# Recurrence of a bidirectional RWKV-7 mixer: turns in quadrants, side work spread over the levels, key factors on GpSimd

## What is computed

```python
def _rwkv_step(S, inp):
    r, w, kk, kka, kt, v = inp
    sk = jnp.einsum('bhij,bhj->bhi', S, kk)
    S = S * w[:, :, None, :] - sk[..., None] * kka[:, :, None, :] + v[..., None] * kt[:, :, None, :]
    return S, jnp.einsum('bhij,bhj->bhi', S, r)
```

## Time and profile before

| | us |
|---|---|
| median of 3 runs | 5085.33 |
| lowest and highest | 5072.62, 5091.82 |
| the profiled execution | 5078.06 |
| its span on the core | 5076.7 |
| TensorE busy | 4573.2 |
| VectorE busy | 1419.8 |
| ScalarE busy | 1174.9 |
| GpSimd busy | 270.6 |

### The profile page before, as it was taken

The page is one execution under the profiler, slowest core; times in us unless marked ns, Lnnn a source line. Parts: engine busy times, 40 slices in busy tenths (PEclk is TensorE's granted clock), DMA queues, the critical chain, the costliest instruction groups (busy, mean ns, idle before and its releaser), DMA issues. The chain is left out here.

```text
span 5076.7 us, 86103 instructions
## 1 busy us (share of the span) xinstructions
PE 4573.2 (90%) x37006; PEld 2463.5 (49%) x37006; DVE 1419.8 (28%) x3516; ACT 1174.9 (23%) x2541; POOL 270.6 (5%) x418
## 2 busy tenths in 40 slices
PE   8999999989998899786999997996888888769998
PEld 6775444434444344543444443444666666534333
DVE  1032110020001221533222225133555555532223
ACT  2032111012101222423222221033333333321111
POOL 0000000000002002102000000022000000010000
PEclk9999999999999899997999998998999999979999
DMA  3143111121122113422777773233000000029998
GB/s 132 67 159 117 66 67 71 66 93 69 66 83 78 50 46 101 139 78 97 294 285 291 285 285 139 91 143 95 28 28 28 28 28 9 3 96 400 407 408 342
DMA packets 257924, 679.81 MB, mean 134 GB/s; under 512 B 23600, under 2 KB 66464, under 8 KB 257296
## 3 DMA queue, kind: packets, MB, share of 16 engines
q1 hardware_dynamic: 234048, 608.24, 32.4%
q0 software_dynamic: 23504, 66.07, 4.3%
HBM read 644.76 MB, written 26.74 MB: 132 GB/s over the span
## 5 line engine op out<-in xcount | busy, mean ns | idle before, releaser
L2197 PE MATMUL bank<-ring,arena 128*128 128x512 f32 x2592 | 1128.8, 596 | 17.1 <-DVE arena L1925 11.3
L2197 PEld LDWEIGHTS bank<-ring,arena 128*128 128x128 f32 x2592 | 559.7, 217 | 562.7 <-issue 477.6
L2566 PE MATMUL bank<-ring,arena 128*64 128x512 f32 x2048 | 470.2, 598 | 9.7 <-DMA ring<-in_moe_w 6.5
L2197 PE MATMUL bank<-arena,ring 128*128 128x512 f32 x1024 | 443.3, 595 | 1.5 <-ACT arena L1157 0.8
L1870 DVE TENSOR_TENSOR arena<-arena,bank 128x512 f32<-128x512 f32 x300 | 187.2, 683 | 649.2 <-PE bank L2539 580.3
L2197 PEld LDWEIGHTS bank<-arena,ring 128*128 128x128 f32 x1024 | 195.3, 191 | 247.1 <-issue 245.0
L2566 PEld LDWEIGHTS bank<-ring,arena 128*64 128x64 f32 x2048 | 139.5, 136 | 311.9 <-issue 308.6
L2592 PE MATMUL bank<-ring,arena 128*64 128x512 f32 x1024 | 232.0, 600 | 2.1 <-ACT arena L1375 1.6
L2368 PE MATMUL bank<-ring,arena 128*128 128x512 f32 x512 | 219.9, 592 | 0.0
L1368 ACT ACTIVATE arena<-bank 64x512 f32<-64x512 f32 x64 | 37.7, 590 | 662.3 <-PE bank L2566 662.3
L2829 PE MATMUL bank<-arena 64*64 64x128 f32 x3840 | 176.3, 302 | 1.0 <-issue 1.0
(11 more groups left out here) (403 smaller groups left out, 5412.2 us busy)
## 6 DMA issues: line engine op xcount, KB each, us to landing
ring<-in_moe_w SPq DMA_DIRECT2D x768, 512.0 KB, 7.5
ring<-in_w_in SPq DMA_DIRECT2D x21, 2048.0 KB, 7.7
ring<-in_ada_w SPq DMA_DIRECT2D x12, 2048.0 KB, 8.0
ring<-in_ada_w SPq DMA_DIRECT2D x24, 1024.0 KB, 5.4
ring<-in_w_up SPq DMA_DIRECT2D x8, 2048.0 KB, 8.1
ring<-in_w_down SPq DMA_DIRECT2D x8, 2048.0 KB, 7.6
ring<-in_na_w_qkv SPq DMA_DIRECT2D x6, 2048.0 KB, 7.9
ring<-in_w_in SPq DMA_DIRECT2D x8, 1024.0 KB, 6.4
```

The source lines that it names most:

```text
L2197: ins = mm(ps[:, 0:ncol], lhs(k), rhs(k), start=(k == 0 and first), stop=(k == nk - 1))
L2566: ins = mm(ps, x_chosen[:, b, k, 0:CAP_L], w[x][:, n * W:(n + 1) * W], start=(k == 0), stop=(k == KD - 1))
```

## The change

- `turn_inverse` and the turns of the factors become 64x64 matmuls against the identity, four quadrants to a 128x128 block, into two banks each. All turns, `y`, group values and nearly all side results now use banks 2 and 3.
- Sums and turns of factors become single jobs (`side`), placed by the table `RW_SIDES` (group, level, kind, direction), ahead of `u` in the level. `rw_scaled` counts their inputs one by one.
- `group_values` stands after the products of level 1, with one result of two banks and two copies; `rw_tgv` and `rw_tk` are one result each.
- In `scan_state` the matmuls of `y` come ahead of the state's. On VectorE `beside_level` puts side work, one or two operations to a level, between the joins and the state's update. `read_out` has six parts.
- `factors` and `weigh_bonus` move from VectorE to GpSimd, written as plain two-input operations: ten of 128x768 and nine of 128x512 for a pair. VectorE keeps the last sum of the bonus.
- The spill tensors are laid out by pair: writes go out in pieces of 512 bytes, and a pair's read is one contiguous piece for each partition. The early load of pair p + 2 is issued between `weigh_bonus(p)` and `factors(p + 1)`.

```diff
+RW_SIDES = [(0, 4, "sum", 0), (0, 5, "sum_ex", 0), (1, 2, "R", 0), (1, 3, "sum", 1), (1, 4, "sum_ex", 1), (2, 2, "K", 0),
+            (2, 3, "B", 0), (2, 4, "T", 0), (2, 5, "R", 1), (2, 5, "K", 1), (2, 6, "B", 1), (2, 6, "T", 1)]
+RW_SCALED = [("R", 0), ("B", 0), ("T", 0), ("K", 0), ("R", 1), ("K", 1), ("B", 1), ("T", 1)]
...
+def rw_scaled(p, kind, z):
+
+    return len(RW_SCALED) * p + RW_SCALED.index((kind, z)) + 1
...
-    def sums(p, z):
-        plan.add("act", "rw_sum", p, z, width=2, bank=0)
-        plan.add("act", "rw_sum_ex", p, z, width=2, bank=2)
-
-    def turn_factors(p, z, *which):
-        for n, x in enumerate(which):
-            plan.add("act", "rw_turn", p, z, x, width=2, bank=turn_bank(z, x))
+    def side(p, kind, z):
+        plan.add("act", "rw_side", p, kind, z, width=2, bank=0 if (kind, z) in (("K", 1), ("T", 1)) else 2)
 
...
     def scan_state(p, i):
+        if i >= 2 * CT:
+            for z in range(2):
+                plan.add("act", "rw_y", p, i, z, bank=2 + z)
         if i + 1 < RW_STEPS:
             for z in range(2):
                 plan.add("dve", "rw_state", p, i, z, bank=z)
-        if i >= 2 * CT:
-            for z in range(2):
-                plan.add("act", "rw_y", p, i, z, bank=2 + z)
...
-                    plan.add("act", "rw_m", p, g, z, lv, bank=2 + z)
+                    plan.add("act", "rw_m", p, g, z, lv, width=2, bank=2)
                     plan.add("act" if lv == RW_LEVELS - 1 else "dve", "rw_x", p, g, z, lv, width=2, bank=4 + 2 * z)
+                if lv == 1:
+                    plan.add("act", "rw_gv", p, g, width=2, bank=2)
+                for job in rw_sides(p, g, lv):
...
-    spill = {q: nc.dram_tensor(f"spill_{q}", [LT if q in "rg" else NT, P, D], F32).ap()
+    spill = {q: nc.dram_tensor(f"spill_{q}", [RW_PAIRS, P, LT if q in "rg" else NT, P], F32).ap()
...
-            pool.dma_start(spill[q][t, :, n * W:(n + 1) * W], staging[:, i % RW_STAGES, :]).then_inc(sem(f"spilled_{i % RW_STAGES}"), 16)
+            pairs = slice(n * W // P, (n + 1) * W // P)
+            pool.dma_start(spill[q][pairs, :, t, :].rearrange("a p d -> p a d"),
+                           staging[:, i % RW_STAGES, :].rearrange("p (a d) -> p a d", d=P)).then_inc(sem(f"spilled_{i % RW_STAGES}"), 16)
...
-                pool.dma_start(RW_IN[q][p % 2], spill[q][:, :, p * P:(p + 1) * P].rearrange("t p d -> p t d")
+                pool.dma_start(RW_IN[q][p % 2], spill[q][p]
...
+        def factors(p):
+
+            I, k_a = {q: v[p % 2] for q, v in RW_IN.items()}, rw_rows[:, p % 2, 1, :]
+            early_landed(pool, p)
+            pool.wait_ge(sem("rw_keys_ready"), p + 1)
+            if p >= 2:
+                full(pool, "rw_y", p - 2, RW_STEPS - 1, 1)
+            for z in range(2):
+                az, B, T = I[f"a{z}"], bh[p % 2][z], th[p % 2][z]
+                link(G.tensor_tensor(T, az, across(k_a, NT), ALU.mult))
+                G.tensor_tensor(B, kk, az, ALU.mult)
+                link(G.tensor_tensor(T, T, across(k_a, NT), ALU.subtract))
+                link(G.tensor_tensor(T, T, I["k"], ALU.mult))
+                G.tensor_tensor(T, T, I["k"], ALU.add).then_inc(sem("rw_factors"), 1)
+
+        def weigh_bonus(p):
+
+            I, k_a, r_k = {q: v[p % 2] for q, v in RW_IN.items()}, rw_rows[:, p % 2, 1, :], rw_rows[:, p % 2, 2, :]
+            w = yd[0]
+            early_landed(pool, p)
+            if p >= 1:
+                pool.wait_ge(sem("rw_bonus_ready"), p)
+            if p >= 2:
+                pool.wait_ge(sem("rw_read_out"), p - 1)
+            link(G.tensor_tensor(w, I["a0"][:, 0:LT], I["a1"][:, 0:LT], ALU.add))
+            link(G.tensor_tensor(w, w, across(k_a, LT), ALU.mult))
+            for _ in range(2):
+                link(G.tensor_tensor(w, w, across(k_a, LT), ALU.subtract))
+            link(G.tensor_tensor(w, w, I["k"][:, 0:LT], ALU.mult))
+            for _ in range(2):
+                link(G.tensor_tensor(w, w, I["k"][:, 0:LT], ALU.add))
+            link(G.tensor_tensor(w, w, I["r"], ALU.mult))
+            G.tensor_tensor(w, w, across(r_k, LT), ALU.mult).then_inc(sem("rw_bonus_weighed"), 1)
+
+        factors(0)
+        for p in range(RW_PAIRS):
+            weigh_bonus(p)
             if p + 2 < RW_PAIRS:
-                pool.wait_ge(sem("rw_bonus_ready"), p + 1)
+                pool.wait_ge(sem("rw_bonus_weighed"), p + 1)
+                pool.wait_ge(sem("rw_scaled"), rw_scaled(p, "R", 1))
+                full(pool, "rw_side", p, "sum_ex", 1)
                 load_early(p + 2)
-            if p >= 1:
+            if p + 1 < RW_PAIRS:
+                factors(p + 1)
+            if 1 <= p < RW_PAIRS - 1:
                 pool.wait_ge(sem("rw_read_out"), p)
                 load_late(p + 1)
         taken(pool, "rw_ot", RW_PAIRS - 1)
@@ -1409,25 +1460,26 @@
             act.wait_ge(sem("rw_kk_squared"), p + 1)
...
+        def side(p, kind, z):
+
+            ps = full(act, "rw_side", p, kind, z)
+            if kind == "sum":
+                if z == 0:
+                    act.wait_ge(sem("rw_kk_squared"), p + 1)
+                if 2 * p + z:
+                    before = (p, "R", 0) if z else (p - 1, "R", 1)
+                    full(act, "rw_side", *before)
+                    act.wait_ge(sem("rw_scaled"), rw_scaled(before[0], "T", before[2]))
+                A(flat(e_neg), ps[:, 0:SEQ], ACT.Exp, scale=-1.0)
+                ins = A(flat(e_pos), ps[:, 0:TOK], ACT.Exp)
+            elif kind == "sum_ex":
+                A(flat(kh[p % 2][z]), ps[:, 0:TOK], ACT.Exp, scale=-1.0)
+                ins = A(w_end[p % 2][z], ps[:, TOK:TOK + RW_STEPS], ACT.Exp, scale=-1.0)
+            else:
+                to, nt = {"K": KT[z], "B": BT[z], "T": TT[z], "R": RT[p % 2][z]}[kind], LT if kind == "R" else NT
+                ps = two_banks(ps, nt * CH).rearrange("p c (t s) -> p c t s", t=nt)
+                ins = A(to.rearrange("p (t c s) -> p c t s", c=2, s=CH), ps, ACT.Copy)
+            free(ins, "rw_side", p, kind, z)
...
+                    if lv == 1:
+                        ps = two_banks(full(act, "rw_gv", p, g), W)
+                        for c in range(2):
+                            rows = slice(c * CH, (c + 1) * CH)
+                            ins = A(gv[rows].rearrange("p z j d -> p (z j d)"), ps[rows, c], ACT.Copy)
+                        free(ins, "rw_gv", p, g)
...
+            to = {"R": e_neg, "K": kh[p % 2][z], "B": bh[p % 2][z], "T": th[p % 2][z]}[kind]
+            taken(dve, "rw_side", p, "sum_ex" if kind == "K" else "sum", z)
+            if kind in "BT":
+                dve.wait_ge(sem("rw_factors"), 2 * p + z + 1)
+            by = {"R": I["r"], "K": kk, "B": e_pos, "T": e_pos}[kind]
+            if kind == "K":
+                dve.wait_ge(sem("rw_keys_ready"), p + 1)
+            scaled[0] += 1
+            assert scaled[0] == rw_scaled(p, kind, z), (p, kind, z)
+            V.tensor_tensor(to, to, by, ALU.mult).then_inc(sem("rw_scaled"), 1)
...
+        READ_OUT = [(1, 1), (1, 3), (1, 4), (1, 5), (2, 1), (2, 2)]
+        KEYS = [(0, 1), (0, 2), (0, 3), (0, 4)]
+        SCALE = {(0, 5): [("R", 0)], (1, 2): [("B", 0), ("T", 0)], (1, 4): [("K", 0)], (2, 2): [("R", 1)], (2, 3): [("K", 1), ("B", 1)],
+                 (2, 4): [("T", 1)]}
+
+        def beside_level(p, g, lv):
+
+            if (g, lv) == (0, 5):
+                sum_bonus(p)
+            if (g, lv) in KEYS and p + 1 < RW_PAIRS:
+                unit_keys(p + 1, KEYS.index((g, lv)) + 1)
+            if (g, lv) in READ_OUT and p >= 1:
+                read_out(p - 1, READ_OUT.index((g, lv)) + 1)
+            if p + 1 < RW_PAIRS:
+                for kind, z in SCALE.get((g, lv), ()):
+                    scale(p + 1, kind, z)
...
+        def side(p, kind, z):
+
             lam = RW_IN[f"w{z}"][p % 2]
...
+            else:
+                x = {"K": kh[p % 2][z], "B": bh[p % 2][z], "T": th[p % 2][z], "R": e_neg}[kind]
+                nt = LT if kind == "R" else NT
+                ps = two_banks(ps, nt * CH)
+                pe.wait_ge(sem("rw_scaled"), rw_scaled(p, kind, z))
+                for t in range(nt):
+                    for hd, c, to, rows in quadrants:
+                        ins = mm(ps[to, c, t * CH:(t + 1) * CH], x[rows, t, to], ident[rows, rows], start=True, stop=True)
...
-            ps = open_("rw_m", p, g, z, lv)
+            ps = two_banks(open_("rw_m", p, g, z, lv), P)
             for j in range(RW_TILES):
-                ins = turn(ps[:, j * P:(j + 1) * P], inv[z][:, j].rearrange("p h s -> p (h s)"), ident[:, :])
+                for hd, c, to, rows in quadrants:
+                    ins = mm(ps[to, c, j * CH:(j + 1) * CH], inv[z][rows, j, hd, :], ident[rows, rows], start=True, stop=True)
...
+                    if lv == 1:
+                        group_values(p, g)
+                    for job in rw_sides(p, g, lv):
+                        side(*job)
```

290 lines of the change are left out of this document (99 added, 191 removed).

## The result

The changed kernel takes **5035.96 us** (median of 4 runs, 5030.97 to 5046.98), the kernel before 5086.31: ratio 0.9915, 95% interval 0.9897 to 0.9932. It is faster, by 50 us (43 by the ratio). The forecast was 4942, its range ended at 5030: 94 us too much was booked as gain. The profiled execution took 5046.98 us (span 5045.7), the slowest of the four; a second base, taken with the experiments, has 5033.23 us and ratio 0.9907 [0.9890, 0.9923].

The account below looks back on a forecast made before the run. No engine fills the recurrence; the chain of waits through TensorE's program order bounds it, 120.6 us a pair. Gains of 169 us, less 38 for GpSimd, plus 5 ahead, net 136 off 5078: 4942 us, range 4880 to 5030.

Parts of the forecast that it names:

- Turns in quadrants: Turns of the inverse in the recurrence: shorter as quadrants, less a wait for shared banks; net gain 4.5 us a pair.
- Turns of the factors: Factor turns, ten to a stretch in TensorE's chain: quadrants cut 9.1 us to 5.1, gaining 4.0 us a pair.
- y ahead of the state: End of a level: state matmuls cover ScalarE's copy of y, for which the next turn waits; gain 1.6 us a pair.
- Sums: Sums between levels: spread over four levels behind the products, the wait for ScalarE's end goes; gain 2.2 us a pair.
- Group values: Level 1 of a group: the turn's 1.15 us wait for ScalarE's four copies goes, three groups; gain 3.5 us a pair.
- VectorE lumps: Joins waiting for VectorE, 4.1 us a pair: work moves to GpSimd or is split over levels; gain 4.0 us a pair.
- Clock: TensorE's granted clock of 0.94 in the recurrence: fewer waits raise it; gain 3.0 us a pair, ends 0 and 5.9.
- GpSimd's lock: VectorE operations with both inputs in SBUF wait while GpSimd runs: loss of 5 us a pair, ends 0 and 25.5.
- Ahead of the pairs: Spill writes, spill reads and the start, before the recurrence's pairs: 5 us of gain for all three, ends -12 and +8.

Follow-up runs that it names:

- vector_factors: The changed kernel with the factors and the bonus back on VectorE, spread over the levels, GpSimd only issuing transfers: 5015.94 us, ratio 0.9879.
- combined: The changed kernel with full-array turns of inverse and factors, factors and bonus on VectorE, and the old spill layout: 4947.87 us, ratio 0.9740.
- full_both: The changed kernel with both the inverse and the factors turned by full-array matmuls again: 4969.84 us, ratio 0.9784.

## Why the prediction was wrong, step by step

**Turns in quadrants, booked as +4.5 us a pair: the step that failed.** Three parts of it were wrong. "0.23 + 0.46 = 0.69" was taken for both turns of a level, but only the first product gets a neighbour of its own tile; the second stands in front of u, whose tiles are 128x64, and takes 0.58 us. The wait for the bank was put at 0.2 us: turn to turn is 1.04 us, not 0.89, and the second wait that the wider reservation makes, behind y, was not seen at all. And the extra instructions, 14 records more for each turn, were priced at nothing, though TensorE then waits for them. Measured: 14 us lost in the kernel before, 28 in the changed one, where a gain of 36 was booked: **64 us of the 94**, give or take 12. By the waits of the two profiles, the 28 us, 3.5 a pair, are 2.4 of gaps for instructions and 1.8 of waits for ScalarE's copies, less 0.8 that waits for VectorE then take; this split is read from the traces, no run makes it.

The Trainium skill has a rule that would have warned: "TensorEngine Tiling (Array Packing)", Restrictions, says that column tiling disables the transpose mode for fp32 operands. The trace agrees: a full-array turn of a tile is one record, the same turn in quadrants is four plain matmuls of two records each, 8 for 1. The prediction used the doubling for the time and overlooked what it does to the number of instructions.

**Turns of the factors, booked as +4.0 a pair.** Set at 0.23/16 us a record, 2.5 us a direction. In the trace six tiles, 48 records, take 0.86 us to the next start where 0.69 was priced, and to it come the gaps in front of L2729, 16.4 us in five pairs, 3.3 of the 4.0 booked. With full-array turns in the same places the kernel is 34 us faster. What the term as a whole gave was not run; by its gaps and its longer records, little. With both kinds of turns full-array the change gives 4970 us, inside the stated range and 28 above the forecast.

A stretch of the changed kernel shows how such a gap looks (timeline, TensorE):

```profile
3950.44 1.23 PE L2729 MATMUL bank<-ident,arena 64*64 64x64 f32 x66
3955.45 0.46 PE L2729 MATMUL bank<-ident,arena 64*64 64x64 f32 x14 [3.78 <-issue]
3955.73 0.75 PE L2896 MATMUL bank<-arena 64*64 64x64 f32 x32
3956.36 2.32 PE L2729 MATMUL bank<-ident,arena 64*64 64x64 f32 x79
3959.41 0.71 PE L2729 MATMUL bank<-ident,arena 64*64 64x64 f32 x17 [0.73 <-issue]
```

The gap opens in the middle of one line's matmuls, 66 after it began: no semaphore stands there. The reads of the next inputs were under way since 3943.6.

**y ahead of the state, +1.6: right as far as can be told** (12 us booked, 12 measured with 12 of uncertainty, and the waits beside it).

**Sums, +2.2: right by the trace; no run undid it.** One direction's sums now take 1.45 us (3898.87 to 3900.32) and 2.69 us (3904.33 to 3907.02) out of the chain, 4.14 in place of 5.18:

```profile
3898.87 1.53 PE L2717 MATMUL bank<-ring,arena 128*128 128x512 f32 x4
3900.32 0.44 PE L2747 MATMUL bank<-arena 128*64 128x128 f32 x4
...
3904.33 1.53 PE L2717 MATMUL bank<-ring,arena 128*128 128x512 f32 x4
3905.70 1.40 PE L2721 MATMUL bank<-arena,ring 128*128 128x2 f32 x12
3907.02 0.44 PE L2747 MATMUL bank<-arena 128*64 128x128 f32 x4
```

**Group values, +3.5: over half of it shows.** The wait for ScalarE's four copies is gone; level 1 of the last group takes 6.97 us (3916.39 to 3923.36) in place of 7.61, so 0.64 of the 1.15, and two waits of 0.29 and 0.43 us for VectorE's operations of the group's start (L2090, L2098) are in it. No run undid it alone.

**VectorE lumps, +4.0: right, but not for GpSimd's sake.** The joins wait 0.4 us for VectorE in the whole kernel, where it was 30.7. With the factors back on VectorE, spread over the levels, they wait 0 and 0.6 us (vector_factors, combined): the spreading earned the term, and the move to GpSimd was not needed for it.

**Clock, +3.0: direction right.** 0.97 in place of 0.94, and 0.99 in the combination; no run isolates its price.

**GpSimd's lock, -5 a pair, 38 in all: too high.** Undoing it gives 14 us on the changed kernel and 22 on the one with full-array turns, net of what VectorE's own operations then cost. Where it lies is told only roughly, by single profiles. From the first sums to the clearing of pair 1 it is 3645.7 - 3463.2 = 182.5 us in the changed kernel and 3638.7 - 3468.1 = 170.6 in vector_factors, and a pair is 1 us shorter there; from full_both to its twin without GpSimd it is 169.9 and 160.1, and a pair is 3.3 us shorter. Two profiles of one kernel (combined) differ by 7 us in that first stretch. So 1 to 3 us a pair instead of 5, and some 10 us in the start and pair 0, which the charge did not single out. One such case in the pairs:

```profile
3930.32 3.10 DVE L2052 SCALAR_TENSOR_TENSOR arena<-arena 128x128 f32<-128x128 f32 x2
...
3930.80 1.29 POOL L1150 TENSOR_TENSOR ring<-ring 128x512 f32<-128x512 f32 x1
...
3932.17 1.09 POOL L1151 TENSOR_TENSOR ring<-ring,arena 128x512 f32<-128x512 f32 x1
...
3933.47 0.43 PE L2747 MATMUL bank<-arena 128*64 128x128 f32 x3 [0.47 <-DVE arena L2052]
```

Two scalings take 3.10 us, with two of GpSimd's operations inside that time, where they took 0.61; u pays 0.47, the chain having 2 us of slack to swallow the rest. Operations with one input in PSUM are untouched, as assumed: the joins' subtraction takes 289 ns before and after. The Trainium skill, "SBUF — State Buffer", SBUF: two separate sides, names the operations of VectorE with two SBUF inputs among those that take the lock against GpSimd's reads; the trace agrees: those grew, and those with one input in PSUM did not.

**Ahead of the pairs, +5: wrong in sign.** The writes, put at 0 to 8 us of loss, and the reads, at 5 of gain, come to nothing measurable; the start, put at 5 us of gain, lost 7.5 in its stage. The scale of the first factors waits 6.5 us for GpSimd's last operation, and six scales of 128x768 take 1960 ns each:

```profile
L2021 DVE TENSOR_TENSOR arena<-arena 128x768 f32<-128x768 f32 x6 | 11.4, 1960 | 8.9 <-POOL arena L1139 6.5 <-ACT arena L1477 2.4
```

**In sum.** Of the 94 us the inverse's turns are 64. The factors' turns are up to 28 more, all that was booked for them, and the start about 12. The lock goes the other way: 38 charged, 14 to 22 measured, the start's part in it. These do not add to 94 exactly; each difference carries its 12 us. The combination, which drops the quadrants, GpSimd's operations and the new spill, reaches 4948 us. That this is close to the number forecast for the change is a coincidence: it lacks gains that the forecast booked and a charge that it made.

## What to carry to other kernels

Before replacing one large operation of TensorE by several small ones, count the records, not only the microseconds: a full-array transpose of fp32 was one record here, its four quadrants eight, and TensorE used them up faster than they came. Look in TensorE's waits for "issue" gaps inside one line's matmuls, in the queue of instructions for its bytes, and whether a gap ends shortly after one of its packets lands; together they tell it. Take the price of a step from rows with the same neighbours, on both sides, and when a reservation gets wider, list every user of each bank in it.

## What the runs showed of the hardware

Each record that TensorE got more, matmul or weight load, brought 64 bytes through the instruction queue: (5.64 - 4.90) MB / (2 x 5,824) = 63.5. The packets are 16 KB, and all 301 gaps without a named releaser between 3640 and 4215 us, in 17 profiles, end 1.19 to 1.65 us after one has landed. TensorE stalls so for up to 5.0 us at a time, above all where such records come dense: 6.3 to 7.8 us a pair with all turns in quadrants, 2.4 and 4.9 with one kind of them, 1.2 to 2.3 with none, 8.3 when one kind is doubled, and 0.4 where more long transposes of 0.11 to 0.12 us stand between. With the reads of the inputs cut to one row they were 6.2, a seventh less than in the changed kernel beside it.

A matmul's time to the next start depends on that neighbour: 16 of 64x128 in 64x64 tiles take 0.44 us in front of matmuls in the same tiles (six times in the changed kernel) and 0.58 in front of tiles of 128x64 (nine times).
